# Two decoder layers written out one after the other, with one loop over rounds of experts

## What is computed

```python
for l in range(DEPTH):                          # DEPTH = 2
    h = rms_norm(x, norm1_g[l])
    r_q, r_k, r_v, r_g, m_q, m_k, m_v, c_q = split(h @ w_in[l])
    y_ret  = silu(r_g) * rms_norm(retention(rotary(r_q), rotary(r_k), r_v))
    y_moba = moba_attention(rms_norm(m_q), rms_norm(m_k), m_v)     # causal, blocks of 256
    mem_kv = rms_norm(mem, mem_norm_g[l]) @ w_mem_kv[l]            # mem: 256 rows
    y_mem  = memory_attention(rms_norm(c_q), *mem_kv)
    x = x + concat(y_ret, y_moba, y_mem) @ w_out[l]
    x = x + hier_moe(rms_norm(x, norm2_g[l]))   # top group of 4, then top 2 of its 4 experts
```

## Time and profile before

| | us |
|---|---|
| median of 3 runs | 1258.1 (1255.04 to 1259.31) |
| profiled execution, its own time | 1256.25 |
| its span (first to last instruction) | 1254.6 |
| PE busy in the span | 1144.6 (91%) |
| DVE busy | 897.5 (72%) |
| ACT busy | 698.4 (56%) |

### The profile page before, as it was taken

How to read it: one execution, slowest core, us unless ns; L and a number is a source line. 1 busy time by engine, 2 the same in 40 slices (tenths; PEclk the granted TensorE clock), 3 DMA queues, 4 the chain that set the end, 5 groups by cost and what they waited for, 6 DMA issues and landing times.

```text
span 1254.6 us, 18217 instructions
## 1 busy us (share of the span) xinstructions
PE 1144.6 (91%) x5538; PEld 917.3 (73%) x5538; DVE 897.5 (72%) x1288; ACT 698.4 (56%) x968; POOL 186.5 (15%) x238
## 2 busy tenths in 40 slices
PE   4999998999999999999279999989999999999991
PEld 3887676788777887777168876667877788877770
DVE  5467555637988988988194675556489888988973
ACT  6322322324888888887252223324248888888860
POOL 3005001001012212211400050010011212222211
PEclk9999799999999999999679997999999999999996
DMA  9522211206999979997943222112089997999965
GB/s 341 185 82 67 68 34 34 68 34 249 365 368 351 358 266 377 369 361 295 340 147 102 69 66 68 34 35 84 34 296 375 373 371 270 344 365 381 364 241 213
DMA packets 121892, 277.46 MB, mean 221 GB/s; under 512 B 13265, under 2 KB 13473, under 8 KB 121680
## 3 DMA queue, kind: packets, MB, share of 16 engines
q1 hardware_dynamic: 106912, 240.30, 53.1%
q0 software_dynamic: 14896, 36.19, 8.0%
HBM read 269.56 MB, written 23.07 MB: 233 GB/s over the span
## 4 chain that ended last, share of the span: by engine, by line
PE 70%; DMA 11%; DVE 9%; issue 5%; ACT 3%; POOL 1%; POOLq 0%; ACTq 0%; DVEq 0%
PE bank L1386 19%; PE bank L1388 18%; PE bank L1387 18%; DMA xg<-h_scratch,tok_now 5%; DMA pair_rows<-ysb,pair_now 5%; PE bank L1418 3%; PE bank L1490 2%; PE bank L1717 2%; PE bank L1511 1%; PE bank L1517 1%; PE bank L1485 1%; DMA hd<-pair_rows 1%; PE bank L1575 1%; DVE w_lo L390 1%; DVE x L925 1%
## 5 line engine op out<-in xcount | busy, mean ns | idle before, releaser
L386 DVE TENSOR_TENSOR w_lo<-stage,w_hi 128x1024 fp32r<-128x1024 f32 x244 | 294.0, 1220 | 16.0 <-ACT w_hi L381 14.5
L381 ACT ACTIVATE w_hi<-stage 128x1024 fp32r<-128x1024 f32 x236 | 246.4, 1059 | 48.0 <-PE bank L1388 48.0
L1386 PE MATMUL bank<-w_hi,hT_hi 128*128 128x512 f32 x384 | 157.5, 410 | 4.5 <-DVE hT_lo L939 4.5
L1388 PE MATMUL bank<-w_hi,hT_lo 128*128 128x512 f32 x384 | 152.6, 397 | 0.0
L1387 PE MATMUL bank<-w_lo,hT_hi 128*128 128x512 f32 x384 | 152.5, 397 | 0.0
L386 DVE TENSOR_TENSOR more_lo<-stage,more_hi 128x1024 fp32r<-128x1024 f32 x124 | 146.0, 1218 | 1.8 <-ACT more_hi L381 1.4
L381 ACT ACTIVATE more_hi<-stage 128x1024 fp32r<-128x1024 f32 x124 | 127.9, 1060 | 15.0 <-PE bank L1388 14.5
L349 ACT ACTIVATE w_hi<-stage 128x1024 fp32r<-128x1024 f32 x56 | 58.8, 1057 | 113.9 <-PE bank L1388 113.9
L390 DVE TENSOR_TENSOR w_lo<-stage,w_hi 128x1024 fp32r<-128x1024 f32 x56 | 67.9, 1220 | 74.9 <-ACT w_hi L349 73.9
L1386 PE MATMUL bank<-w_hi,xgT_hi 128*128 128x512 f32 x264 | 104.7, 396 | 1.2 <-DVE xgT_lo L1282 1.2
L1387 PE MATMUL bank<-w_lo,xgT_hi 128*128 128x512 f32 x264 | 104.9, 397 | 0.0
(11 more groups left out here) (239 smaller groups left out, 2009.5 us busy)
## 6 DMA issues: line engine op xcount, KB each, us to landing
stage<-in_w_exp_up SPq DMA_DIRECT2D x124, 512.0 KB, 5.8
stage<-in_w_exp_gate SPq DMA_DIRECT2D x122, 512.0 KB, 5.6
stage<-in_w_exp_down SPq DMA_DIRECT2D x122, 512.0 KB, 6.2
stage<-in_w_in SPq DMA_DIRECT2D x40, 512.0 KB, 4.2
stage<-in_w_out SPq DMA_DIRECT2D x16, 512.0 KB, 3.9
stage<-in_w_mem_kv SPq DMA_DIRECT2D x8, 512.0 KB, 7.5
h_scratch<-act POOLq DMA_DIRECT2D x8, 512.0 KB, 2.9
act<-pair_rows POOLq DMA_DIRECT2D x8, 512.0 KB, 6.2
```

The source lines that it names most:

```text
L381: eng.activation(x_hi[n % NX], src, ACT.Copy).then_inc(s_hi, 1)
L386: eng.tensor_tensor(x_lo[n % NX], src, x_hi[n % NX].bitcast(f32), ALU.subtract).then_inc(s_lo, 1)
L1386: pe.matmul(dst, l_hi, r_hi, start=start, stop=False)
L1388: return pe.matmul(dst, l_lo, r_hi, start=False, stop=stop)
```

## The change

1. On all engines the loop over layers is a Python loop: the code of a layer stands twice, for layer 0 and layer 1, with fixed addresses for the layer's weights. The tests on the layer number (`If(layer > 0)` and the like) are gone.
2. On ACT, DVE, PE and GpSimd the experts stand once in each layer, in `Fori(0, rounds)`, where `rounds` is a register that is 1 at the start and is set to the real number inside the loop. What differs in a later round stands in `If(r > 0)` with an `Else` of one empty instruction. All rounds now treat the first expert's rows with the code that round 1 had. SP keeps its form (a first pass, and others behind `If(rounds > 1)`).
3. After the last layer SP and not GpSimd issues the eight loads of `pair_rows`, on eight semaphores of their own (`s_yl`). Between the layers GpSimd does it, as before.
4. In attention, ACT's `make_hi` of unit 27 stands behind `evacuate(4)`, and ahead of that stands a Silu of one column (`tint`). DVE's `make_lo` of that unit stands in the sixth retention step (`r == 5`).

```diff
@@ sync
-            with sp.Fori(0, DEPTH) as layer:
+            for layer in range(DEPTH):
...
-                flat[0] = sp.snap(layer * E_N)
+                flat[0] = layer * E_N
...
+            for t in range(2):
+                sp.wait_ge(s_yst[t], sp.snap(passes, min_val=1, max_val=NT * DEPTH) * 128 + 16 * t)
+            apart(sp)
+            for q in range(2 * NT):
+                r0 = SEQ * (q % 2) + 128 * (q // 2)
+                sp.dma_start(y_rows[q], y_d[r0:r0 + 128, :]).then_inc(s_yl[q], 16)
             for t in range(NT):
                 sp.wait_ge(s_x, 16 * DEPTH + 4 * (t + 1))
@@ gpsimd
-            with pool.Fori(0, DEPTH) as layer:
+            for layer in range(DEPTH):
...
-                with pool.If(layer > 0):
+                if layer > 0:
                     load_results()
-                with pool.Else():
-                    pool.nop()
...
-                    if first:
+                    with pool.If(r > 0):
+                        gather_dma(0, slot_tok[:, 0:1])
+                    with pool.Else():
                         pool.dma_start(spare[:, :], a["const_pack"][0:16, 0:2]).then_inc(s_xg[0], 16)
-                    else:
-                        gather_dma(0, slot_tok[:, 0:1])
                     gather_dma(1, slot_tok[:, 1:2])
-                    if first:
-                        pool.wait_ge(s_known, 1)
-                        rounds = rounds_of(pool)
+                    pool.wait_ge(s_rounds, layer + 1)
+                    apart(pool)
+                    pool.reg_mov(rounds, rounds_of(pool))
...
-                rounds = experts(True)
-                with pool.If(rounds > 1):
-                    with pool.Fori(1, rounds) as r:
-                        experts(False)
-                with pool.Else():
-                    pool.nop()
-            load_results()
@@ scalar
-                    if j in FREED_AT:
+                    if j in FREED_AT and j < 23:
                         make_hi(sc, base, 20 + FREED_AT[j])
                     if j == 5:
                         evacuate(3)
+                sc.activation(tint[:, :], eps, ACT.Silu)
                 evacuate(4)
+                make_hi(sc, base, 20 + FREED_AT[23])
...
-                def experts(first):
+                sc.reg_mov(rounds, 1)
+                with sc.Fori(0, rounds) as r:
...
-                    if not first:
+                    with sc.If(r > 0):
                         for n in range(NW):
                             expert_hi(sc, base_p, n)
+                    with sc.Else():
+                        sc.nop()
@@ vector
-                make_lo(dv, base, 20 + FREED_AT[23])
                 tile_out(3)
...
+                    if r == 5:
+                        make_lo(dv, base, 20 + FREED_AT[23])
...
-                def experts(first):
+                dv.reg_mov(rounds, 1)
+                with dv.Fori(0, rounds) as r:
...
             for t in range(NT):
-                combine(16 * DEPTH, t)
+                combine(s_yl, 16, t)
@@ tensor
-                def experts(first):
+                pe.reg_mov(rounds, 1)
+                with pe.Fori(0, rounds) as r:
...
-                    if first:
-                        pe.wait_ge(s_half_l, 1)
-                        gate_up(0, base_p, 0, 0, 4)
-                        pe.wait_ge(s_xgl, 1)
-                        gate_up(0, base_p, 4, 4, 2)
-                    else:
-                        turn_rows(0, p2 * 128 + 16)
-                        pe.wait_ge(s_xgl, 1)
-                        gate_up(0, base_p, 0, 0, 6)
+                    with pe.If(r > 0):
+                        pe.wait_ge(s_xg[0], p2 * 128 + 16)
+                        apart(pe)
+                        for k in range(KT):
+                            ins = pe.transpose(...)
+                            if k % 4 == 3:
+                                ins.then_inc((s_half_t, s_xgt)[k // 4], 1)
+                    with pe.Else():
+                        pe.nop()
+                    pe.wait_ge(s_half_l, 1)
+                    gate_up(0, base_p, 0, 0, 4)
+                    pe.wait_ge(s_xgl, 1)
+                    gate_up(0, base_p, 4, 4, 2)
                     turn_rows(1, p2 * 128 + 16)
```

More of the change, by code:

```diff
@@ L478, in _ @@
                     load(base, n, of(a["w_mem_kv"], 256 * n, 0))
-                with sp.If(layer < 1):
+                if layer == 0:
                     for t in range(NT):
@@ L598, in _ @@
                 pool.wait_ge(s_slot, 1)
-                def experts(first):
+                pool.reg_mov(rounds, 1)
+                with pool.Fori(0, rounds) as r:
                     p = pool.snap(passes, min_val=0, max_val=NT * DEPTH)
@@ L676, in _ @@
             per_unit = 16 // NS
+            rounds = sc.alloc_register("act_rounds")
             def ring():
                 return sc.snap(loaded, min_val=0, max_val=per_unit * DEPTH * (U_ATT + NT * U_PASS))
-            with sc.Fori(0, DEPTH) as layer:
+            for layer in range(DEPTH):
                 p = sc.snap(passes, min_val=0, max_val=NT * DEPTH)
@@ L895, in experts @@
                     hidden_hi(E_N)
-                    if first:
-                        sc.wait_ge(s_known, 1)
-                        rounds = rounds_of(sc)
+                    sc.wait_ge(s_rounds, layer + 1)
+                    apart(sc)
+                    sc.reg_mov(rounds, rounds_of(sc))
                     results(E_N, 0, end[0], U_FIRST + U_E + FT)
@@ L903, in experts @@
                     sc.reg_add(passes, passes, 1)
-                    return rounds if first else None
-                rounds = experts(True)
-                with sc.If(rounds > 1):
-                    with sc.Fori(1, rounds) as r:
-                        experts(False)
-                with sc.Else():
-                    sc.nop()
         @block.vector
@@ L929, in combine @@
                         dv.sem_inc(s_x, 4)
-            with dv.Fori(0, DEPTH) as layer:
+            for layer in range(DEPTH):
                 p = dv.snap(passes, min_val=0, max_val=NT * DEPTH)
@@ L967, in norm_x @@
                     norm(act[:, t, :], x[:, t, :], 2 + t, s_h1, g_norm1)
-                steps = chain.n
-                with dv.If(layer > 0):
-                    before = dv.snap(layer * 16, min_val=16, max_val=16 * DEPTH)
-                    for t in range(NT):
-                        combine(before, t)
-                        if t:
-                            norm_x(t - 1)
-                with dv.Else():
-                    chain.n = steps
-                    for t in range(NT):
+                for t in range(NT):
+                    if layer > 0:
+                        combine(s_yg, layer * 16, t)
+                    else:
                         dv.wait_ge(s_xin[t], 16)
                         dv.sem_inc(s_x, 4)
-                        if t:
-                            norm_x(t - 1)
+                    if t:
+                        norm_x(t - 1)
                 norm_x(NT - 1)
@@ L1419, in turn @@
                 ins.then_inc(s, 1)
-            with pe.Fori(0, DEPTH) as layer:
+            for layer in range(DEPTH):
                 p = pe.snap(passes, min_val=0, max_val=NT * DEPTH)
@@ L1781, in experts @@
                     down(E_N, end, U_FIRST + U_E)
-                    if first:
-                        pe.wait_ge(s_known, 1)
-                        rounds = rounds_of(pe)
+                    pe.wait_ge(s_rounds, layer + 1)
+                    apart(pe)
+                    pe.reg_mov(rounds, rounds_of(pe))
                     slot_table(bank[5][:, 0:E_N * VALS], s_tail_at, 1, s_tail_tab)
@@ L1788, in experts @@
                     pe.reg_add(passes, passes, 1)
-                    return rounds if first else None
-                rounds = experts(True)
-                with pe.If(rounds > 1):
-                    with pe.Fori(1, rounds) as r:
-                        experts(False)
-                with pe.Else():
-                    pe.nop()
 _INS = ["x", "mem", "norm1_g", "w_in", "ret_norm_g", "moba_qn_g", "moba_kn_g", "mem_norm_g", "w_mem_kv", "mem_qn_g",
```

77 lines of the change are left out of this document (36 added, 41 removed).

## The result

The changed kernel takes 1280.5 us (median of four runs, 1272.1 to 1288.6) where the kernel before, on the same chip, takes 1257.0 (1255.0 to 1259.3). The ratio is 1.0185, 95% interval 1.0102 to 1.0269: 1.9% slower. I had forecast 1235.9 us and given "slower" 3 in 100. The profiled execution of the kernel after took 1272.1 us with a span of 1270.3, against 1254.6 before: 15.7 us more.

The account below looks back on a forecast made before the run. PE was taken as busy within the experts, leaving its gaps elsewhere to gain from. 12.3 + 6.5 + 3.4 = 22.2 us off 1256.25 gave 1234.05; with 1.85 for the median, 1235.9 us, range 1230 to 1243.

Parts of the forecast that it names:

- the first one: Experts: PE is busy there and the change touches nothing that repeats, so gains were sought in PE's gaps elsewhere.
- the section on what is added: Costs of the new `If`, a table load and register steps, mostly at the experts' start: 0, at most 1 us.
- The rival on the slower side: Experts: a pair loop no longer fits in what PE holds; its jumps back cost up to 71 us; chance 0.02.
- The boundary: Between the layers: far jumps go and DVE's norm then waits for the gain vector; 12.3 us gained, bounds 9.6 and 13.5.
- Attention's end: Last attention tile in each layer: both 3.2 us waits of PE go; 6.5 us gained, bounds 4.1 and 7.
- The tail: After the last expert: SP's loads bring earlier combines, eight in 10.9 us; 3.4 us gained, bounds 0.6 and 3.9.
- The sum: Whole kernel: boundary, attention and tail gains together, 22.2 us.
- The added `If`: Start of the experts: a near branch taken once a layer on four engines, within a cost taken as 0.

Follow-up runs that it names:

- e11: Kernel before with only the layers written out and the single loop over rounds; 1251.7 us, ratio 0.9936.
- e10: Kernel before with only the last expert rows loaded by SP; 1254.3 us, ratio 0.9973.
- e4: Kernel before with GpSimd issuing the gather ahead of its wait for the scatter's landing; 1251.9 us, ratio 0.9969.
- e8: Kernel before with only attention's last weight unit split later, the early silu writing the old tile `warm`; 1249.9 us, ratio 0.9930.
- e1: Kernel after without the tile `tint`, the early silu writing the old tile `warm`; 1238.8 us, ratio 0.9873.
- e5: Kernel after with 32 unused bytes declared ahead of `xgT_hi`; 1235.1 us, ratio 0.9837.

## Why the prediction was wrong

- **The step that failed** is the first one: "Within the experts PE is busy and the change touches nothing that repeats there." The change touches where the experts' tiles lie. In the section on what is added I listed instructions and took 0; the declaration of `tint` in the diff is none of these, so it had no line in the sum. It is worth 40 us: 1.0185 / 0.9873 = 1.032. What the runs showed in its place: PE waits 32.1 us for gathered rows instead of 3.5 and has half its clock for 30.7 us around these waits, against 10 us won by the faster beat.
- **The chances.** The rival on the slower side was a stall of the pair loops' jumps, which never came. The place was right, the experts; the mechanism wasn't among the rivals. The profile of before held a hint: gathers on GpSimd just in time, with PE's 3.5 us of waits for them, the scatter's landing ahead of each, and VectorE's rows of low parts beside them. The prediction doesn't take these 3.5 us up. They said that the gathers had next to no slack.
- **The boundary, 12.3 us:** PE's wait fell by 21.7 - 10.5 = 11.2 in the profile, within the bounds of 9.6 and 13.5. The far jumps were the cause and the gain vector is the next bound. Counted from the start of the last results (`ysb`), the norm came at 9.3 us where I had put 613.6 - 605.34 = 8.3: the vector took 5.9 us from issue to landing, not 5. `mem` is close behind as a bound: ScalarE began its squares 4.4 us behind `ysb`, and VectorE was ready for the norm at 8.5, 0.8 us ahead of the vector. Alone (e11) the part gave 8.0, interval 5 to 11; its profile has the wait at 10.3, but from the norm to the experts it took 315.1 us, before 311.1. TensorE's clock goes with that: it was at half for 47.5 us of this stretch, before for 40.4. In e10 and e4, unchanged there, the stretch took 315.2 and 314.6 us with 47.9 and 47.5 at half. So the 4 us go with the clock of single executions; whether the written-out layers make them likelier isn't shown.
- **Attention's end, 6.5 us:** 8.8 measured, interval 6 to 12; I had put the upper bound at 7. Both waits are gone as worked out. The sum left out the clock: before, it fell to half for 3.4 us at 212.39 and at 833.61, half a us before the two waits ended, and the 16 transposes behind the first took 3.36 us; in e8 the clock stays at full there and they take 1.9.
- **The tail, 3.4 us:** 3.4 measured (e10), interval 0 to 7, too wide to confirm it. The trace of after has 3.7 us to the first combine and 12.4 for the eight, where I had put 3.9 and 10.9, because loads and stores still overlap. From the last results to the end it is 2.6 us shorter than before (28.3 and 25.6), and 0.9 of that is a scatter that landed sooner. That 3.4 came out is in part luck.
- **The sum, 22.2 us:** with the experts' tiles on their old places it is 16 (e1) or 20.5 (e5), so 1238 to 1242 us from the median of 1258.1; the range of 1230 to 1243 holds it. The added `If` costs 0.23 us a layer and needed no more.
- **Still open:** why the place of `xgT` and `hidT` sets the beat, and what decides whether GpSimd gets its turn at a boundary. The runs show that both happen, and that a gap settles the second.

## What to carry to other kernels

A tile that a change declares is part of the change: write down which tiles behind it move and by how much, or declare it last, and try the empty declaration by itself before crediting or blaming the rest. Where a small wait recurs in the hot loop, follow it back: a gather that is just in time, behind another transfer's landing and beside an unbroken row of VectorE work, can turn a gain elsewhere into a loss. A wait of TensorE of 3 us and more may cost more than its length: look at the granted clock behind it. Moving the gather's issue ahead of that landing was worth more here (about 55 us) than all three edits together. And look whether a wait put in as an experiment can hold at all: read the count that its semaphore starts from.

## What the runs showed of the hardware

- 32 unused bytes changed TensorE's beat: 512-column fp32r matmuls started every 233.2 to 233.5 ns with the stationary tiles on odd multiples of 32 bytes, 229.2 to 229.3 on odd multiples of 64, and 227.6 to 227.7 on multiples of 128 (means; unbroken rows of the last kind 226.7).
- GpSimd's indirect DMA, 1.0 to 1.9 us as a rule, took 4.0 to 5.2 us when VectorE ran up to four two-input instructions of 1.13 us without a gap. The same phase gave both. A gap of 0.14 us, which moved the next start by 0.22, was enough. With the slow beat the same phase never gave a long one, in 96 cases.
- Around each of TensorE's seven waits of 3.6 to 4.6 us in the experts of after, the granted clock was at half for 3.4 or 6.8 us, and 512-column matmuls started every 427 ns instead of 229. In the kernels without such waits it stayed at full there.
- A taken branch that skips a copy of the experts cost 3.9 to 5.3 us; one over eight transposes 0.23 us.
